# Decay sums spread by DMA, one z tile among the last chunk's products, states stored in parts, value groups at other tiles

## The reference

```python
def gdn_chunk(S, xs):
    q, k, v, g, beta = xs
    G = jnp.cumsum(g, axis=-1)
    decay = jnp.exp(jnp.where(incl, G[..., :, None] - G[..., None, :], -jnp.inf))
    a_mat = jnp.where(strict, beta[..., :, None] * jnp.einsum('bhid,bhjd->bhij', k, k) * decay, 0.0)
    ...
    qk = jnp.einsum('bhid,bhjd->bhij', q, k) * decay
    o = jnp.einsum('bhck,bhkv->bhcv', q * jnp.exp(G)[..., None], S) + jnp.einsum('bhij,bhjv->bhiv', qk, v_new)
    ...

def sb_sample(q, k_new, v_new, cache_k, cache_v, page_table, bias):
    kp = cache_k[page_table].reshape(b, past, HB, DH_B)
    vp = cache_v[page_table].reshape(b, past, HB, DH_B)
    ...
    return (jnp.einsum('bhqk,bkhd->bqhd', a[..., :past], vp)
            + jnp.einsum('bhqk,bkhd->bqhd', a[..., past:], v_new))
```

## Time and profile before

| | |
|---|---|
| median of 3 runs | 1443.67 us (1440.56 to 1444.44) |
| the profiled execution | 1448.45 us |
| its span in the trace | 1446.7 us, 27991 instructions |
| PE busy | 1360.6 us, 94%, 10626 matmuls |
| PEld busy | 1242.6 us, 86% |
| DVE busy | 798.2 us, 55% |
| ACT busy | 516.2 us, 36% |
| POOL busy | 198.9 us, 14% |
| DMA | 261.35 MB, mean 181 GB/s |

### The profile page before, as it was taken

How to read it: one execution, slowest core, us unless ns; L and a number is a source line. 1 busy time by engine, 2 the same in 40 slices (tenths; PEclk the granted TensorE clock), 3 DMA queues, 4 the chain that set the end, 5 groups by cost and what they waited for, 6 DMA issues and landing times.

```text
span 1446.7 us, 27991 instructions
## 1 busy us (share of the span) xinstructions
PE 1360.6 (94%) x10626; PEld 1242.6 (86%) x10626; DVE 798.2 (55%) x2972; ACT 516.2 (36%) x787; POOL 198.9 (14%) x290
## 2 busy tenths in 40 slices
PE   6998989899989989988998899999999999999998
PEld 5997966678988868767886788898999999999998
DVE  4688739867988757576544422344544343332322
ACT  4323345636845222233223342223342222222222
POOL 1000002223220533200330000000111111110100
PEclk9999999999999989897999999999999999999998
DMA  9469848644533488779679999442333333332332
GB/s 312 146 230 303 287 152 276 236 146 150 158 98 92 133 288 298 287 275 269 181 226 329 305 318 300 136 148 59 90 95 94 88 95 96 88 94 86 95 91 75
DMA packets 255370, 261.35 MB, mean 181 GB/s; under 512 B 22561, under 2 KB 215211, under 8 KB 254437
## 3 DMA queue, kind: packets, MB, share of 16 engines
q1 hardware_dynamic: 255237, 259.57, 55.7%
HBM read 240.05 MB, written 19.68 MB: 180 GB/s over the span
## 4 chain that ended last, share of the span: by engine, by line
PE 75%; issue 7%; DVE 5%; DMA 4%; SPq 3%; ACT 3%; POOL 2%; POOLq 0%; ACTq 0%; DVEq 0%
PE ps L1112 59%; PE ps L1146 4%; DMA wring<-in_w_in 1%; SPq L752 1%; POOL R L2860 1%; PE ps L1436 1%; PE ps L1595 1%; PE ps L1421 1%; DVE kring L2296 1%; PE ps L1455 1%; PE ps L1490 1%; DMA wring<-in_cache_k 1%; PE ps L1478 1%; PE ps L1440 1%; DMA xn<-in_cache_v 1%
## 5 line engine op out<-in xcount | busy, mean ns | idle before, releaser
L1112 PE MATMUL ps<-obT_split,wring_split 128*128 128x268 f32 (+2 forms) x1296 | 264.3, 285 | 0.0
L1112 PE MATMUL ps<-obT_split,qv_split 128*128 128x260 f32 (+2 forms) x1040 | 218.9, 292 | 4.6 <-DVE wring_split L616 3.0
L1112 PEld LDWEIGHTS ps<-obT_split,wring_split 128*128 128x128 f32 (+1 forms) x1296 | 201.3, 189 | 0.5
L1112 PE MATMUL ps<-obT_split,vring_split 128*128 128x260 f32 (+1 forms) x960 | 196.7, 286 | 0.8 <-issue 0.8
L616 DVE TENSOR_TENSOR wring_split<-wring,vring_split 128x1024 fp32r<-128x1024 f32 (+1 forms) x92 | 118.0, 1283 | 138.6 <-ACT vring_split L610 138.6
L1112 PE MATMUL ps<-xn_split,vring_split 128*128 128x260 f32 (+1 forms) x960 | 193.2, 282 | 0.0
L1112 PE MATMUL ps<-xn_split,qv_split 128*128 128x260 f32 (+2 forms) x912 | 186.4, 286 | 0.0
L1112 PEld LDWEIGHTS ps<-obT_split,qv_split 128*128 128x128 f32 (+1 forms) x1040 | 162.1, 190 | 24.9 <-issue 22.5
L616 DVE TENSOR_TENSOR wring_split<-wring,qv_split 128x1024 fp32r<-128x1024 f32 (+1 forms) x73 | 90.9, 1245 | 135.5 <-ACT qv_split L610 135.4
L1112 PEld LDWEIGHTS ps<-obT_split,vring_split 128*128 128x128 f32 x960 | 147.9, 188 | 3.0 <-issue 2.6
L1112 PEld LDWEIGHTS ps<-xn_split,vring_split 128*128 128x128 f32 x960 | 148.0, 188 | 0.1
(11 more groups left out here) (413 smaller groups left out, 2171.4 us busy)
## 6 DMA issues: line engine op xcount, KB each, us to landing
wring<-in_w_in SPq DMA_DIRECT2D x72, 512.0 KB, 5.5
kring<-in_cache_k SPq DMA_DIRECT2D x64, 512.0 KB, 5.2
wring<-in_w_ffn_in SPq DMA_DIRECT2D x44, 512.0 KB, 3.8
vring<-in_cache_v SPq DMA_DIRECT2D x40, 512.0 KB, 5.2
kring<-in_cache_v SPq DMA_DIRECT2D x40, 512.0 KB, 5.6
vring<-in_cache_k SPq DMA_DIRECT2D x24, 512.0 KB, 5.8
R<-in_cache_k SPq DMA_DIRECT2D x24, 512.0 KB, 7.1
obT<-in_cache_v SPq DMA_DIRECT2D x24, 512.0 KB, 5.5
```

The lines of the kernel that those rows point to most:

```text
L1112: last = mm(ps[0:m, 2 * (t % 2) + i, 0:n], fr(w), fr(x[k][:, a + i * n:a + i * n + n]), start=(k == 0 and w is w_h and x is hi), stop=(k = ...
```

## The change

- **Decays.** The cumulative sums of all chunks are transposed once on PE (`cumulative_rows`, tile 6 of s=0), copied by ACT and stored to DRAM (`gdram`). SP loads each chunk's row spread over the partitions (`decay_rows` at s=2, `decay_columns` in the chunks). POOL subtracts it and the column and masks with a large negative number, ACT takes the exponential in place. The matmuls of lines 1265 and 1386 go, and so do the products of line 2932. In the convolution stage POOL's and ACT's steps stand one head later.
- **Last chunk.** The convolution rows stand among the products of chunk 4, in two banks by turns; the first z tile stands ahead of the last outputs, its weights split behind chunk 3's work (high part in `kring`). Key page 15 goes ahead of these two loads.
- **Stores.** The states are stored two parts at s=5, j=7, one at s=6, j=0 and one at s=6, j=1. The gates over the DeltaNet output move from s=6 to s=7.
- **Groups.** `QUAD_TILES` is another list: 42, 43, 44, then 47 to 59, then 61 to 64.

```diff
...
+    if p == T_Z:
+        return "kr", 2
...
-CHUNK_ORDER = ["ks", ("q1", 32), "ot", "vn", ("up", 32), "qs", "kv", ("q1", 64), "o2", "dc", ("up", 64), "tk", "kq", "tv"]
-HEAD_PAIR = {("q1", 32): 2, "tk": 3, "dc": 1, ("up", 32): 0, ("q1", 64): 2, ("up", 64): 0, "tv": 3, "kq": 2}
+CHUNK_ORDER = ["ks", ("q1", 32), "ot", "vn", ("up", 32), "qs", "kv", ("q1", 64), "o2", ("up", 64), "tk", "kq", "tv"]
...
-QUAD_TILES = dict(zip(range(N_EARLY, N_QUAD), (43, 44, 46, 47, 48, 49, 51, 52, 53, 54, 55, 57, 58, 60, 61, 62, 63, 65, 66, 67)))
+QUAD_TILES = dict(zip(range(N_EARLY, N_QUAD), (42, 43, 44, 47, 48, 49, 50, 51, 52, 53, 54, 55, 56, 57, 58, 59, 61, 62, 63, 64)))
...
+        gT = rows[0:H * TT, 0:P]
+        gdram = nc.dram_tensor("gdram", [TT, D], F32).ap()
...
+                if n == N_EARLY + 1:
+                    sp.wait_ge(w_used, done(T_Z))
...
+            def decay_rows(c, dst):
+
+                n = chunk(c)
+                return sp.dma_start(dst[0:n, :, 0:n], gdram[c:c + 1, :].rearrange("a (h j) -> a h j", h=H)[:, :, 0:n]
+                                    .to_broadcast([n, H, n]))
+
+            def decay_columns(c):
+
+                if c == 0:
+                    sp.wait_ge(k_used, K_CHUNKS)
+                elif c == 1:
+                    sp.wait_ge(g_pool, POOL_AT[0, ("L", 64), 1])
+                else:
+                    sp.wait_ge(g_pe, PE_AT[c - 2, "o2", 1])
+                decay_rows(c, DC[c % 2]).then_inc(dc_in[c % 2], 16)
...
-                sp.wait_ge(g_pe, PE_AT[4, "dc", 1])
+                sp.wait_ge(g_pe, PE_AT[3, ("up", 64), 1])
...
-                    if s == 6 and j == 0:
-                        for i in range(4):
-                            store_states(i)
+                    for i in {(5, 7): (0, 1), (6, 0): (2,), (6, 1): (3,)}.get((s, j), ()):
+                        store_states(i)
...
                     if (s, j) == (0, 7):
+                        sp.wait_ge(ab_a, 12)
+                        sp.dma_start(gdram.rearrange("c (h j) -> (c h) j", h=H), gT).then_inc(rows_out, 16)
                         store_keys(0)
                     if (s, j) == (1, 3):
                         store_keys(1)
+                    if s == 2 and j in (1, 2):
+                        if j == 1:
+                            sp.wait_ge(rows_out, 32)
+                        for c in ((0, 1), (2, 3, 4))[j - 1]:
+                            decay_rows(c, DR[c]).then_inc(row_in, 16)
...
+                    decay_columns(0)
                     chunk_query()
                     chunk_pages(0, 3)
                     get_inverse(1)
+                    decay_columns(1)
...
                     v_quad(11)
+                    decay_columns(4)
                     chunk_pages(12, 15)
                     last_inverse()
                     late_page(1)
+                    chunk_pages(15, PAGES)
                     sp.wait_ge(ob_out, 16 * 5)
                     sp.wait_ge(v_used, N_EARLY - 1)
                     sp.dma_start(obT2[:, :, :], nhdram[:, :, :]).then_inc(x_in[0], 16)
                     sp.wait_ge(v_used, N_EARLY)
                     sp.dma_start(xn2[:, :, :], nldram[:, :, :]).then_inc(x_in[0], 16)
-                    chunk_pages(15, PAGES)
                     late_page(2)
...
-            def conv_rows(a, b):
-
-                pe.wait_ge(raw_c, NQKV)
-                for n in range(4 * a, 4 * b):
-                    m = tr(ps[0:11, (0, 1, 2, 3, 6, 7)[n // 4], (n % 4) * P:(n % 4) * P + P], rawt[:, n, :], ident[:, :])
-                    if n % 4 == 3:
-                        m.then_inc(co_t, 1)
-                if b == 6:
-                    pe.wait_ge(co_c, 4)
-
-            def decay_blocks(c):
-
-                n = chunk(c)
-                pe.wait_ge(gm_ok, c + 1)
-                if 1 <= c < 4:
-                    pe.wait_ge(dr_ex, 2 * c)
-                for g in G2:
-                    o = ps[0:n, 5, 64 * g:64 * g + 64] if c == 4 else ps[0:n, 6 + g, 0:4 * n]
-                    mm(o, tri_le[0:n, 0:n], gms[c % 2][0:n, 4 * g:4 * g + 4, 0:n], start=True, stop=True)\
-                        .then_inc(dr_mm, 1)
+            def conv_row(i):
+
+                if i == 0:
+                    pe.wait_ge(raw_c, NQKV)
+                    pe.wait_ge(ob_s, V_EARLY)
+                if i >= 2:
+                    pe.wait_ge(co_c, i - 1)
+                for n in range(4 * i, 4 * i + 4):
+                    m = tr(ps[0:11, 6 + i % 2, (n % 4) * P:(n % 4) * P + P], rawt[:, n, :], ident[:, :])
+                m.then_inc(co_t, 1)
...
+            def cumulative_rows():
+
+                pe.wait_ge(ab_a, 11)
+                tr(ps[0:H * TT, 7, 0:P], tmp1, ident[:, :]).then_inc(ab_m, 1)
...
-                def decay_columns(c):
-
-                    n = chunk(c)
-                    after("pool", c, "gm")
-                    if not c:
-                        wait_read(pe, T_SEG + 5 * KT - 2)
-                    for g in G2:
-                        if c:
-                            after("dve", c - 1, "S", g)
-                        for h in heads(g):
-                            m = mm(place(c, "dc", h, n), gm[0:n, h, 0:n], tri_le[0:n, 0:n], start=True, stop=True)
-                        m.then_inc(g_pe, 1)
...
                 for c in range(TT):
                     d = c + 1
+                    if d == TT:
+                        conv_row(0)
+                        conv_row(1)
                     if c:
                         state_products(c, "ks")
                     level_first(d, 32)
...
                     if c:
                         outputs(c - 1)
                     new_values(c)
+                    if d == TT:
+                        conv_row(2)
+                        conv_row(3)
...
-                pe.wait_ge(ob_s, V_EARLY)
-                after("dve", TT - 1, "o", 1)
-                conv_rows(0, 4)
+                conv_row(4)
+                conv_row(5)
+                pe.wait_ge(x_in[0], 16 * 4)
+                after("dve", TT - 1, "S", 1)
+                tile_split(T_Z, n_hi, n_lo, a=first_token(T_Z))
...
+                    if T_SEG + s * KT + j == T_Z:
+                        pass
...
-                    if 2 <= u <= 5:
-                        decay_blocks(u - 2)
-                    if u == 5:
-                        decay_blocks(4)
...
+            def decay_exps(c, dst, sig):
 
                 n = chunk(c)
                 for g in G2:
-                    act.wait_ge(dr_mm, 2 * TT if c == 4 else 2 * c + g + 1)
-                    src = ps[0:n, 5, 64 * g:64 * g + 64] if c == 4 else ps[0:n, 6 + g, 0:4 * n]
-                    go(DR[c][0:n, 4 * g:4 * g + 4, 0:n], src.rearrange("p (h j) -> p h j", h=4), ACT.Exp)\
-                        .then_inc(dr_ex, 1)
+                    d = dst[0:n, 4 * g:4 * g + 4, 0:n]
+                    go(d, d, ACT.Exp).then_inc(sig, 1)
+
+            def decay_blocks(c):
+
+                act.wait_ge(dr_ok, 4 * c + 4)
+                decay_exps(c, DR[c], dr_ex)
...
+                nc.scalar.copy(tmp1, ps[:, 7, 128:168]).then_inc(ab_a, 1)
+
+            def cumulative_rows():
+                act.wait_ge(ab_m, 2)
+                act.wait_ge(rows_out, 16)
+                nc.scalar.copy(gT, ps[0:H * TT, 7, 0:P]).then_inc(ab_a, 1)
...
+                    after("pool", c, "cm", 1)
+                    decay_exps(c, DC[c % 2], g_act)
...
+                    if c == TT - 1:
+                        after("pe", 3, ("q1", 64), 1)
+                        split_hi(act, T_Z)
...
+                        if (s, j) == (7, 0):
+                            act.wait_ge(zs_done, 1)
+                            act.wait_ge(z_done, KT)
+                            act.wait_ge(r_out, 16 * 5)
                         read_tile(t, (sgA if s == 6 else sgB)[:, j, :], ACT.Sigmoid)
-                        if s == 6:
-                            if j == 0:
-                                act.wait_ge(zs_done, 1)
-                                act.wait_ge(z_done, KT)
-                                act.wait_ge(r_out, 16 * 5)
+                        if s == 7:
                             gate_hi(oa_hi[j], oa_full[j])
...
+                def conv_rows(a, b):
+                    for i in range(a, b):
+                        dve.wait_ge(co_t, i + 1)
+                        v.tensor_copy(convrow_sb[0:11, i, :], ps[0:11, 6 + i % 2, :]).then_inc(co_c, 1)
...
+                    if not more:
+                        conv_rows(0, 4)
...
+                    if not more:
+                        split_lo(dve, T_Z)
...
+                    if not more:
+                        conv_rows(4, 6)
...
                     if s == 6:
                         late(6, j)
+                    if s == 7:
                         gate_lo(dve, KT + j, oa_hi[j], oa_full[j], oa_lo[j])
...
+            def decay_mask(c):
 
                 n = chunk(c)
```

(36 more changed lines are left out.)

94 lines of the change are left out of this document (32 added, 62 removed).

## The result

The changed kernel took 1449.39 us (median of 13 runs, 1444.85 to 1455.77), the kernel before, run beside it, 1442.71 (13 runs, 1438.0 to 1445.3). The ratio is 1.0040, 95% interval 1.0026 to 1.0054: slower by 0.4%, where 1427 was forecast. The profiled execution took 1444.85 us.

The account below looks back on a forecast made before the run. PE, the matmul engine, was taken to bound the kernel, so only removed work or closed gaps count. Terms -6.5 - 5.4 - 9 + 4 = -16.9, applied to the median 1443.67, gave 1427 us; range 1413 to 1438.

Parts of the forecast that it names:

- Part 1: Convolution stage: decay sums taken off PE (20 matmuls, 8.0 us); forecast -6.5 us, bounds -8.7 and 0.
- late next: Convolution stage: ScalarE's logs for PE's key norms, behind GpSimd's steps and the exponentials; charged 2.2 us, between 0 and 8.7.
- Rival (a): Convolution stage: VectorE or the inverse's chain sets its end, longer wait for inverses; sum -10.4, 1433 us; chance 0.12.
- Part 2: Chunks: decay columns without 80 PE matmuls (9.5 us); forecast -5.4 us, bounds -11 and 0.
- Before chunk 0 the 3.1 us go: Ahead of chunk 0: removed decay matmuls at the low clock, some 3.1 us, were to be saved.
- The first value group, issued no earlier, holds the gain: Start of the chunks: the first value group's unchanged issue limits the saving before chunk 0 to about 3 us.
- the fifth load's wait: Chunks: SP held by the fifth load until chunk 2's second product, three key pages behind it; claimed to cost nothing.
- Part 3: Last chunk: key page earlier, convolution copies into waits, z tile into waiting time; forecast -9 us, bounds -16 and -2.
- new wait: Ahead of the second z tile: 4 to 8 us for ScalarE's split behind the final state's store, tile at 667.
- Part 4: Late value groups, state stores and gates, tiles 48 to 59 mainly: forecast +4 us, bounds -6 and +12.
- The rule of the Trainium skill: Late value groups: about 358 GB/s of HBM per core, giving -4 instead of +4, sum 1419; not taken as limit.
- Rival (d): Tiles 49 to 59: every late value group late, 6.3 us each; with five further ones 1454 us, slower; chance 0.08.

Follow-up runs that it names:

- the second trace: The changed kernel, no edit, traced again beside the kernel before: traced execution 1447.88 us, median of ten runs 1446.99 us, ratio 1.0034.
- the second trace of before: The kernel before, no edit, traced again: 1440.39 us (one run).

## Why the prediction was wrong, point by point

- **Part 1, the step that failed.** "The 8.0 us lie in a stretch where PE is nearly full, so they are on the path." They were not: PE's slack to the chain of key pages, weight tile and ScalarE's log was 0.4 to 1.5 us, and GpSimd's longer steps made a second chain of the same length. The charge of 2.2 (bound 8.7) for "late next" measured 7.3, and the bounds left out what comes behind such a wait. Tile 21 started 4 us early, tile 24 2 us late and tile 39 5 us late, with a granted clock of 0.95 for 0.98; where the clock came back (two traces of five) tile 39 was 0.1 and 0.8 late, still no gain. Rival (a) had the mechanism, an engine other than PE that sets the stage's end, with its place and its price of 0 wrong.
- **Part 2.** "Before chunk 0 the 3.1 us go": they went into the wait for ScalarE at L1337 (1.9 before, 5.3 and 5.7 after). "The first value group, issued no earlier, holds the gain": it was issued 8 us later. Some 5 of these are tile 39's, from part 1; with that part undone the group goes out at 505.1 and 504.1, still 3 to 4 us late, because GpSimd's subtractions stand ahead of the buffer that SP's load waits for. I had followed only the fifth load's wait. The early groups then took 8.7 us of waits, not 6 to 7, in five places. Sum 0.2 to 0.4 for -5.4, above the bound of 0.
- **Part 3 was right in size and in its new wait.** -7.8 and -8.4 for -9, and alone 0.53% of the whole time, 7.6 us; the store of the final state was forecast to leave behind the states' loads and the second z tile at 667. It left at 655.34, landed 9.8 us later, and the tile started at 667.7. The reason was off: PE's gaps in the stretch hardly shrank (9.2 to 8.0), the granted clock rose from 0.75 to 0.90. I had given the clock 1 us. Some of it came back: tiles 41 to 47 took 3.5 to 7.8 us more in every kernel with this part, at 0.90 to 0.96 where the kernel before has 1.00. PE's gaps there are the same 1.3 us before and in both traces of the changed kernel, so these us are the clock's alone. I had no term for that. That the low clock only moved there is the reading that fits; no run tested it.
- **Part 4.** +4.7 and +4.4 for +4, waits of 7.1, 2.8 and 5.0 us at tiles 49, 50 and 53 for 6 to 7, 2 to 3 and 3 to 4. Right as a sum. That the groups at 42 to 44 cost nothing and the rest a few us was too little for the list alone, if the stretch from tile 48 is taken (7.5), and near if tiles 41 to 47 are counted in (3.5 to 5). The rule of the Trainium skill (DMA: Bandwidth & Descriptors, Specifications) would have made this term a gain of 4; the trace shows a loss, and 388 GB/s from 580 to 600 us in the changed kernel, above the page's limit.
- **The base.** The terms were applied to the median, rightly, but read from a trace with a low-clock stretch of its own.

Against the second trace the forecast missed by 25.7 us (8.8 + 16.9): 11.9 are part 1, 5.8 part 2, 5.0 the tiles 41 to 47, 3 the rest. Against the medians it is 22.4; the second trace of before lies 2.3 below its own. Of the 11.9, 6.5 is the gain that wasn't there, in every trace, and 5.4 the loss, nearly all of it low clock that two traces don't have. Rival (d) named late groups as the way to a slower kernel, at five more waits; there were two more in the first trace and one in the second. The kernel became slower because parts 1 and 2 gave nothing, while what part 3 gave went to part 4, to tiles 41 to 47 and to the low clock behind part 1's wait.

## What to carry to other kernels

PE being 94% busy doesn't make every matmul worth its time. Before counting a removed matmul, follow from each place where PE would arrive early to what must be there: the weight tile, the queue position ahead of it, the engine that frees that queue. Count the slack: a chain that runs 0.4 us beside PE makes no wait, and no list of waits shows it. Charge the clock for a wait that appears, as a range. Where one profile lies off the median of its kernel, trace it twice before it becomes a base.

## What the hardware showed that I had not expected

**Waits and the clock.** The same wait of some 3 us, for the same value group near 590 us, was followed by the full clock in one trace of the same kernel and by the low level in the other (the two windows above), and this alone moved a run by 5 us. The wait of 7.2 to 7.7 us in the convolution stage did the same to tile 39, five traces of the same code falling into 482.2 to 482.9 and 486.3 to 487.5. It may be why ten runs of one kernel span 12 to 18 us here; that wasn't tested.

**GpSimd holds VectorE up.** VectorE's key products take 0.28 us, but not beside GpSimd's subtractions. VectorE, changed kernel:

```profile
347.75 1.12 DVE L2315 CUSTOM_DVE_ANT_0 kring<-kring,qv 128x128 f32<-128x128 f32 x1
...
350.49 0.70 DVE L2315 CUSTOM_DVE_ANT_0 kring<-kring,qv 128x128 f32<-128x128 f32 x1
...
351.12 0.28 DVE L2315 CUSTOM_DVE_ANT_0 kring<-kring,qv 128x128 f32<-128x128 f32 x1
```

and GpSimd:

```profile
347.63 2.14 POOL L2961 TENSOR_TENSOR R<-small,R 128x512 f32<-128x512 f32 x2
349.73 1.32 POOL L2886 TENSOR_SCALAR_AFFINE_SELECT R<-R 128x512 f32<-128x512 f32 x2
```

Four products from 347.75 to 351.12 take 3.4 us, the next four, alone, 0.85. The Trainium skill (SBUF — State Buffer, SBUF: two separate sides) says that the two engines share a pair of ports which one instruction holds to its end, when VectorE reads two operands from SBUF; these rows agree. The kernel before shows the same beside its GpSimd products, but less of it: there only three of these products are long (0.71, 0.70 and 0.47 us). So VectorE, which began them 0.9 us earlier in the changed kernel than in the second trace of before, let the two key pages go 0.4 us later (352.56 for 352.17), and the weight tile behind them.
